# Modulation rows with moving weights, a first product in the setup stage, 64x64 blocks in the delta rule's inverse, and its dense tiles four units later

## The reference, cut to what matters

```
lower = where(strict, einsum('bhncd,bhnmd->bhncm', k_beta, k) * decay, 0.0)
a_mat = lower + eye(C)
sol = triangular_solve(a_mat, concat([v_beta, k_beta * exp(g)]), lower=True, unit_diagonal=True)
u, w = sol[..., :DV], sol[..., DV:]
...
step: v_new = u_i - w_i S;  o_i = q_dec_i S + qk_i v_new;  S = S * gl_i + k_dec_i^T v_new
```

## Time and profile before

| what | before |
|---|---|
| median of three runs | 3587.12 us |
| the profiled execution | 3585.75 us, its span 3583.9 us |
| TensorE (PE) matmuls busy | 3501.8 us, 98% |
| VectorE (DVE), ScalarE (ACT) busy | 1992.3 us (56%), 1233.8 us (34%) |
| mean granted TensorE clock | 0.991 of full speed |

### The profile page before, as it was taken

How to read it: one execution, slowest core, us unless ns; L and a number is a source line. 1 busy time by engine, 2 the same in 40 slices (tenths; PEclk the granted TensorE clock), 3 DMA queues, 4 the chain that set the end, 5 groups by cost and what they waited for, 6 DMA issues and landing times. The chain is left out here.

```text
span 3583.9 us, 43286 instructions
## 1 busy us (share of the span) xinstructions
PE 3501.8 (98%) x17750; PEld 2870.8 (80%) x17750; DVE 1992.3 (56%) x2959; ACT 1233.8 (34%) x1912; POOL 150.0 (4%) x212
## 2 busy tenths in 40 slices
PE   7999999999999999999999999999999999999999
PEld 6888877688888888877688887888888888888887
DVE  5665676775466755676763356665423376562233
ACT  3213334632233223344532234635322264442222
POOL 1110100001000100100000001000000000000000
PEclk8999999999999999999999999999999999999999
DMA  7663341245343653331343332211233222113322
GB/s 267 215 214 113 90 110 48 81 150 191 126 153 117 216 166 120 98 101 43 91 127 118 112 130 60 66 46 62 83 97 120 95 61 71 36 59 113 94 95 88
DMA packets 438042, 397.74 MB, mean 111 GB/s; under 512 B 53780, under 2 KB 390276, under 8 KB 437845
## 3 DMA queue, kind: packets, MB, share of 16 engines
q1 hardware_dynamic: 413028, 310.53, 28.5%
q0 software_dynamic: 24816, 84.45, 6.9%
HBM read 390.14 MB, written 4.78 MB: 110 GB/s over the span
## 5 line engine op out<-in xcount | busy, mean ns | idle before, releaser
L175 PE MATMUL m_ps<-m_h_high,ffn_w_high 128*128 128x512 f32 x2064 | 806.7, 391 | 2.9 <-DVE ffn_w_low L182 2.9
L177 PE MATMUL m_ps<-m_h_high,ffn_w_low 128*128 128x512 f32 x2064 | 803.5, 389 | 0.0
L176 PE MATMUL m_ps<-m_h_low,ffn_w_high 128*128 128x512 f32 x2064 | 803.2, 389 | 0.0
L1006 ACT ACTIVATE ffn_sil<-m_ps 128x512 f32<-128x512 f32 x132 | 79.1, 600 | 1095.1 <-PE m_ps L177 1095.1
L175 PEld LDWEIGHTS m_ps<-m_h_high,ffn_w_high 128*128 128x128 f32 x2064 | 387.5, 188 | 84.3 <-issue 4.3
L177 PEld LDWEIGHTS m_ps<-m_h_high,ffn_w_low 128*128 128x128 f32 x2064 | 387.4, 188 | 81.0
L176 PEld LDWEIGHTS m_ps<-m_h_low,ffn_w_high 128*128 128x128 f32 x2064 | 387.6, 188 | 79.1
L175 PE MATMUL m_ps<-ffn_w_high,ffn_hid_high 128*128 128x512 f32 x1056 | 411.6, 390 | 0.0
L177 PE MATMUL m_ps<-ffn_w_high,ffn_hid_low 128*128 128x512 f32 x1056 | 410.9, 389 | 0.0
L176 PE MATMUL m_ps<-ffn_w_low,ffn_hid_high 128*128 128x512 f32 x1056 | 410.9, 389 | 0.0
L182 DVE TENSOR_TENSOR ffn_w_low<-m_raw,ffn_w_high 128x2048 fp32r<-128x2048 f32 (+1 forms) x138 | 296.3, 2150 | 114.9 <-ACT ffn_w_high L1000 114.9
(11 more groups left out here) (498 smaller groups left out, 5497.6 us busy)
## 6 DMA issues: line engine op xcount, KB each, us to landing
m_raw<-in_ffn_w SPq DMA_DIRECT2D x176, 512.0 KB, 4.7
ffn_rows<-in_ada_w POOLq DMA_DIRECT2D x128, 512.0 KB, 5.1
ffn_rows<-in_ffn_w SPq DMA_DIRECT2D x88, 512.0 KB, 3.5
m_raw<-in_w_in SPq DMA_DIRECT2D x32, 1024.0 KB, 5.2
m_raw<-in_ffn_w_gate SPq DMA_DIRECT2D x44, 512.0 KB, 3.8
m_raw<-in_ffn_w_up SPq DMA_DIRECT2D x44, 512.0 KB, 4.9
ffn_rows<-in_ffn_w_down SPq DMA_DIRECT2D x44, 512.0 KB, 3.4
m_raw<-in_w_out SPq DMA_DIRECT2D x24, 512.0 KB, 4.6
```

The source lines that it names most:

```text
L175: pe.matmul(out, sh, mh, start=first, stop=False, skip_group_check=True)
L176: pe.matmul(out, sh, ml, start=False, stop=False, skip_group_check=True)
L177: return pe.matmul(out, sl, mh, start=False, stop=last, skip_group_check=True)
L1006: act.activation(sil[:, f % 2, :], M.ps[:, 2 * (f % 2), :], ACT.Silu).then_inc(S.silu_done, 1)
```

## The change: what it does

There are three edits in different stages, and one reordering.

1. **setup.** For chunks n = 2 and 3, VectorE sums only the first four slices (`on_dve(n)`). The other four are added by TensorE with the raw modulation weights as the moving operand and c broadcast as the stationary one, 128x512 each (`ada_products`); one more matmul with ones adds VectorE's part (`ada_rest`), ScalarE copies the one row (`copy_row`), and `ada_turn` turns it into columns. Seven tape heads instead of five stand ahead of the transposes. The gate weights of the first ffn tile are loaded after the first chunk's sum, and its first product (both halves, 48 matmuls of 256 columns) is done in setup, slice by slice as h comes; ffn begins with the up tile.
2. **scores** in mixer1_rest alternate between the two groups of rows.
3. **the inverse.** At levels 1 to 5 `first_product` and `updates` multiply only the two 64x64 blocks on the diagonal of each head (16 matmuls of 64x64 with 64 moving columns in place of 4 of 128x128 with 128), at level 6 one 64x64 block a head; copies and subtractions of level 6 are cut to that block, those of other levels stay whole.
4. **the tiles.** Tile n = 4 to 14 stands at unit 2(n - 4) + 5 instead of 2(n - 4) + 1, is evacuated in its own unit, ahead of that unit's `update`, and the last one (n = 15) stands behind the products u and w, its evacuation on ScalarE behind the last copy of w and on VectorE inside the recurrence.

```diff
+            def ada_products(n):
+                pe.wait_ge(ada_landed[2 * n + 1], 16)
+                for k in range(on_dve(n), DT):
+                    pe.matmul(row_bank(n), M.ccol[:, k:k + 1].to_broadcast([P, P]), ada[:, n, k, :], start=(k == on_dve(n)), stop=False)
+            def ada_rest(n):
+                pe.wait_ge(S.ada_partial, n + 1)
+                pe.matmul(row_bank(n), M.ones[:], part[:, n % 3, :], start=False, stop=True).then_inc(S.ada_rows, 1)
...
+            ada_products(2)
+            ada_rest(2)
+            ada_products(3)
             pe.wait_ge(S.mod_chain, 3)
-            ada_column(2)
-            ada_column(3)
+            ada_turn(2)
+            ada_rest(3)
+            keep_running(pe, M, 2, 2)
+            ada_turn(3)
+            pe.wait_ge(S.next_low, 1)
+            pe.wait_ge(S.h_ready, HALF)
+            first_product(range(HALF))
+            for k in range(HALF, DT):
+                if k > HALF:
+                    keep_running(pe, M, 2, 1)
+                pe.wait_ge(S.h_ready, k + 1)
+                first_product([k])
...
-                for h in range(HEADS):
-                    rows = slice(HD * (h // HPG), HD * (h // HPG + 1))
+                for a in range(HPG):
+                    for g in range(GROUPS):
+                        rows = slice(HD * g, HD * (g + 1))
...
+    final = len(sequence) - 1
+    last_unit = {n: 2 * (n - TT) + TT + 1 for n in range(TT, final)}
+    last_unit.update({n: -1 for n in range(TT - 1)})
+    ended = lambda u: [n for n in range(final) if last_unit.get(n) == u]
...
+        HALVES = [slice(0, P // 2), slice(P // 2, P)]
+        corner = lambda ap, h, half: head(ap[HALVES[half]], h)[:, HALVES[half]]
...
+                    elif n < LAST:
+                        for half in range(2):
+                            mm = pe.matmul(corner(out, h, half), corner(A.BT[:, i], h, half), corner(X[:, i], h, half), start=True, stop=True)
...
             for u in range(UNITS + 1):
                 if u < UNITS:
                     first_product(u)
-                if u % 2 and 4 + u // 2 < len(sequence) - 1:
-                    dense(4 + u // 2)
+                for n in ended(u):
+                    dense(n)
                 if u:
                     updates(u - 1)
                 if TT <= u - 2 < UNITS - TT:
                     turn_inverse(u - 2)
-            dense(len(sequence) - 1)
...
+            dense(final)
...
             for i in range(TT):
                 act.wait_ge(S.w_ready, i + 1)
                 act.copy(A.wT[:, i], M.ps[:, first_bank(UNITS + i) + 1]).then_inc(S.w_copied, 1)
...
-                high_gated(i)
+                if i < TT - 1:
+                    high_gated(i)
+            evacuate(final)
+            high_gated(TT - 1)
...
                 if i:
                     gate_output(i - 1)
                 else:
-                    low_gated(TT - 1)
+                    evacuate(final)
```

More of the change, by code:

```diff
@@ L232, in _ @@
             sp.dma_start(M.tri[:], const(nc, triangle(), "c_tri")).then_inc(S.tri_landed, 16)
-            sp.wait_ge(S.ada_partial, 2)
-            ahead.load(sp)
+            for s in range(2):
+                sp.wait_ge(S.ada_partial, s + 1)
+                ahead.load(sp, s)
             sp.wait_ge(S.ada_partial, 4)
@@ L281, in ada_column, with ada_turn, first_product @@
                 mm.then_inc(S.ada_column, 1)
+            def ada_products(n):
[5 more added lines that the diff above has]
+                pe.matmul(row_bank(n), M.ones[:], part[:, n % 3, :], start=False, stop=True).then_inc(S.ada_rows, 1)
+            def ada_turn(n):
+                c = order[n]
+                pe.wait_ge(S.row_copied, n - 1)
+                for q in range(T // P):
+                    mm = pe.matmul(M.ps[:, 7, 4 * c + q:4 * c + q + 1], part[0:1, row_slot(n), q * P:(q + 1) * P], M.ones[0:1, 0:1], start=True, stop=True)
+                mm.then_inc(S.ada_column, 1)
+            def first_product(ks):
+                for half in range(2):
+                    tokens = slice(2 * P * half, 2 * P * (half + 1))
+                    for k in ks:
+                        product(pe, M.ps[:, 0, tokens], (M.early[:, 0, k], M.early[:, 1, k]), (M.h_high[:, k, tokens], M.h_low[:, k, tokens]),
+                                k == 0 and half == 0, k == DT - 1)
             ada_column(0)
@@ L311, in _, with copy_row @@
             tape_copies(range(AT_ONCE, HEADS))
-            high_values(range(DT))
+            def copy_row(n):
+                act.wait_ge(S.ada_rows, n - 1)
+                act.copy(part[0:1, row_slot(n), :], row_bank(n)[0:1, :]).then_inc(S.row_copied, 1)
+            high_values(range(HALF))
+            copy_row(2)
+            ahead.first_high_act(act, M).then_inc(S.next_high, 1)
+            copy_row(3)
+            high_values(range(HALF, DT))
         @block.vector
@@ L2710, in first_product @@
                     pe.wait_ge(S.x_copied, u - 2 * TT + 1)
+                out = M.ps[:, first_bank(u)]
                 for h in range(DH):
-                    if n:
-                        mm = pe.matmul(head(M.ps[:, first_bank(u)], h), head(A.BT[:, i], h), head(X[:, i], h), start=True, stop=True)
-                    else:
-                        mm = pe.transpose(head(M.ps[:, first_bank(u)], h), head(A.BT[:, i], h), M.ident[:])
+                    if n == 0:
+                        mm = pe.transpose(head(out, h), head(A.BT[:, i], h), M.ident[:])
+                    elif n < LAST:
+                        for half in range(2):
+                            mm = pe.matmul(corner(out, h, half), corner(A.BT[:, i], h, half), corner(X[:, i], h, half), start=True, stop=True)
+                    else:
+                        mm = pe.matmul(head(out[HALVES[1]], h)[:, HALVES[0]], head(A.BT[HALVES[0], i], h)[:, HALVES[1]],
+                                       corner(X[:, i], h, 0), start=True, stop=True)
                 mm.then_inc(S.t1, 1)
@@ L2722, in updates @@
                 pe.wait_ge(S.t1_copied, u - TT + 1)
+                out = M.ps[:, first_bank(u)]
                 for h in range(DH):
-                    mm = pe.matmul(head(M.ps[:, first_bank(u)], h), head(T1[:, i], h), head(Y[:, i], h), start=True, stop=True)
+                    if n < LAST:
+                        for half in range(2):
+                            mm = pe.matmul(corner(out, h, half), corner(T1[:, i], h, half), corner(Y[:, i], h, half), start=True, stop=True)
+                    else:
+                        mm = pe.matmul(head(out[HALVES[0]], h)[:, HALVES[1]], head(T1[HALVES[1], i], h)[:, HALVES[0]],
+                                       corner(Y[:, i], h, 1), start=True, stop=True)
                 mm.then_inc(S.x_up, 1)
@@ L2868, in _ @@
                     copy_inverse(u - 2)
-                if u >= 3 and u % 2 and 4 + (u - 3) // 2 < len(sequence) - 1:
-                    evacuate(4 + (u - 3) // 2)
-                if u >= 5 and u % 2 and 2 + (u - 5) // 2 < len(sequence) - 1:
-                    square(2 + (u - 5) // 2)
-            evacuate(len(sequence) - 1)
+                for n in ended(u):
+                    evacuate(n)
+                for n in ended(u - 6):
+                    square(n)
             for i in range(TT):
@@ L2876, in _ @@
                 act.copy(A.wT[:, i], M.ps[:, first_bank(UNITS + i) + 1]).then_inc(S.w_copied, 1)
-                high_gated(i)
+                if i == 0:
+                    for u in range(UNITS - 6, UNITS):
+                        for n in ended(u):
+                            square(n)
+                if i < TT - 1:
+                    high_gated(i)
+            evacuate(final)
+            high_gated(TT - 1)
             act.wait_ge(ahead.landed[0], 16)
@@ L3006, in _ @@
                     mask(u + 2)
+                for n in ended(u):
+                    evacuate(n)
                 update(u)
-                n = 4 + (u - 3) // 2
-                if u >= 3 and u % 2 and n < len(sequence) - 1:
-                    evacuate(n)
-                if u >= 1 and u % 2 and 2 <= n - 1 < len(sequence) - 1:
-                    gated_convolution(n - 1, 0)
-                if u >= 2 and u % 2 == 0 and 2 <= n - 1 < len(sequence) - 1:
-                    gated_convolution(n - 1, 1)
-                if u >= 3 and u % 2 and 2 <= n - 2 < len(sequence) - 1:
-                    gated_convolution(n - 2, 2)
-            evacuate(len(sequence) - 1)
+                for n in ended(u):
+                    split_ahead(n)
+                for part in range(SCCONV):
+                    for n in ended(u - 2 - part):
+                        gated_convolution(n, part)
             def low_gated(c):
```

101 lines of the change are left out of this document (58 added, 43 removed).

## The result

The changed kernel takes 3594.77 us (median of 14 runs, 3588.35 to 3601.59) where the kernel before takes 3587.15 (14 runs, 3579.74 to 3591.49). The medians are 7.6 us apart. The ratio, which uses all runs, is 1.0027, with a 95% interval of 1.0019 to 1.0035: slower by 7 to 13 us. Forecast was 3588, range 3572 to 3622. The profiled execution of the changed kernel took 3588.35 us (span 3586.5), the least of its 14, so its stages are read one by one and not by their sum.

What follows compares the result with a forecast made beforehand. TensorE, busy 98% of the span, was taken as the bound. Per layer +3.6 us, two layers +7.2, opening -3.7, scores -2.5: +1.0 in all, giving 3588 us as the median; range 3572 to 3622.

Steps and rivals of the forecast that it cites:

- case "slower": Whole kernel slower than before, with about 7 us as the limit of telling a change; chance 0.43.
- first transposes to first product u: Delta stage, per layer: -19.7 blocks, +9.0 width changes, +10.0 idle first units, +2.5 clock, -1.5 waits, -1.1 last sum of squares.
- first product u to the stage's end: Delta stage's end: v_new 14.0 us behind first product u instead of 10.2, +3.8; with low_gated(3) together +4.4 us a layer.
- opening, whole kernel: Setup and first ffn tile: up tile starts at 54.7 instead of 58.43, -3.7 us; bounds -6 and +4.
- scores, whole kernel: Alternating row groups in mixer1_rest: sixteen records about 1.0 instead of 1.48 us, eight calls, -2.5 us; bounds 0 and -4.5.
- The blocks and the width: Inverse, per layer: 48 groups at 0.48 instead of 0.89 us, -19.7; 32 width changes at 0.28 us, +9.0.
- The rival that the pairs don't overlap: Inverse, levels 1 to 5: a group takes 0.96 instead of 0.48 us, 38 us more, 3626; chance 0.22.
- the rival of nearly free changes: Inverse: a pair of mode changes costs 0.08 instead of 0.28 us, 13 us less, 3575; chance 0.26.
- The first units: Delta stage's start: first dense tile waits for unit 5's mask, TensorE stands still 10.0 us of 12.1 a layer.
- the 2.5 us charged for the clock: Behind the first units' pauses, five us at half clock lose 2.5 us a layer; bounds 0 and 3.5.
- "-1.5, waits 4.0 against 5.5": Later units: the 1.34 us wait goes, TensorE waits 3.3 us for ScalarE at unit 25 plus 0.7 small; -1.5 a layer.
- The bound of 4 us more: Opening: if the clock stays down, ten matmuls take 17 us, up tile 4 us later, 3596; rival's chance 0.12.

Runs made afterwards that it cites:

- join_regroup: Changed kernel with the delta schedule of before, and in odd units the dense tile behind updates and transposes: 3559.50 us, ratio to before 0.9927.
- shift_only: Kernel before with only the later dense tiles, their evacuation in their own unit and the late last sum of squares, blocks whole: 3612.39 us, ratio 1.0066.
- after_again: The changed kernel run and profiled once more, nothing edited: 3596.28 us, ratio to before 1.0035.
- fillers: Changed kernel plus matmuls of 256 columns that nobody reads in three places where TensorE waits: 3590.54 us, ratio to before 1.0007.
- join_fill: Changed kernel with the delta schedule of before, plus 6 unread matmuls ahead of the 2.92 us wait for ScalarE's copy of unit 24: 3563.81 us, ratio 0.9944.

## Why the forecast came out as it did

The time, 3594.8, lies in the range, in the case "slower" and 7 us above the forecast. By its steps, in microseconds of a layer unless it says otherwise:

| term | forecast | measured |
|---|---|---|
| first transposes to first product u | -0.8 (the sum -19.7 + 9.0 + 10.0 + 2.5 - 1.5 - 1.1) | +0.1, -0.4 |
| first product u to the stage's end | +4.4 | +7.1, +7.2 |
| opening, whole kernel | -3.7 | -4.7 (interval -0.7 to -8.6) |
| scores, whole kernel | -2.5 | -1.8, not told from 0 |

**The blocks and the width.** Right in size: a unit was to take 0.44 + 2 x 0.48 + 0.28 = 1.68 us and takes 1.67. With 0.48 a group, 0.27 is left for the change of width in and out, and join_regroup, with 0.33 for a stretch fewer, bears that out. The rival that the pairs don't overlap is shown wrong, and the rival of nearly free changes too. The Trainium skill's page TensorEngine Tiling (Restrictions and Gotchas, Gotcha 1: PSUM Pressure) says that different row tiles can't access one PSUM bank at the same time; the two corners of a head lie in different rows and in different columns and write to one bank here, in different partitions, and pair by pair a group takes 0.5 us, where with the corners apart it takes 0.7 to 0.8, so the measurement decides against it for this case. The same page's drain at a change of mode (Tiling Modes, Key Properties) agrees, with 0.27 us.

**The first units.** Right: TensorE stands still or works at half clock there, 13.3 us where 12.9 was worked out, and the clock came back 2 us into the first dense tile. That tile took 6.7 us instead of 5.7. So the 2.5 us charged for the clock were too much: 0.4 and 1.0 were paid.

**Later units.** The step "-1.5, waits 4.0 against 5.5" failed. The wait of unit 25 was foreseen at 3.3 us and is 3.60, but with 0.68, 0.52 and twice 0.25 of others, for masks, it makes 5.30, more than the 3.88 of before (1.34, 1.97 and 0.57) and not less. Behind it the last two `updates` took 1.9 us at half clock instead of 1.0, which no term held. The sum of the stretch was nonetheless off by 0.9 and 0.4 us only, and that is luck: 1.1 us too much for the clock in the first units stood against 2.2 too little here.

**The stage's end** is the term that was mis-sized, +4.4 for +7.1. Its mechanism was right: `v_new` behind the roots. Where the clock stayed up, in the first layer of shift_only, both numbers came out, 14.0 us and +4.3. What was left out is the clock behind the wait of unit 25. The prediction charged lower clock to the first units alone; in the changed kernel the first three groups of products behind this wait took 4.8 us instead of 2.7. That is 14.0 + 2.1 = 16.1, the measured distance. From `v_new` to the end it is 1.3 us longer than before, 0.7 more than the 0.6 in the sum; a third stretch at half clock lies there, but no run separates it. The two layers make 5.5 us, and with the 0.9 and 0.4 above 6.8: the delta stage alone accounts for all that the forecast was short. Opening and scores together came near their sum of -6.2 (-6.5 by the ratios, with about 4 us of scatter each).

**The opening.** The bound of 4 us more did not come true in any profile; in the first profile the clock was up from 31 us on at the latest, so all ten matmuls ran at full speed, where about half of them had been charged at half; after_again shows the assumed case, with the up tile at 55.19, near the 54.7 of the prediction. So the term was too small in most executions: on average of the profiles the up tile starts 6.4 us earlier, not 3.7. A window that the prediction didn't read points to the reason: before, the clock was at 0.99 from 28 to 31 us, behind the transposes, and was at 0.50 from 31 us on, with the three tape heads and the pauses behind them. The changed kernel has one head there. That this is why the clock stays up in some executions and not in others isn't shown.

What stays open: the ratios of single parts carry about 4 us of scatter each, so whether opening and scores keep their full gain beside the other parts isn't shown. The delay's cost is split only by stretches of one trace (8.2 and 4.3 us), not by a run with the dense tiles delayed and the last sum of squares ahead of u and w, since that sum needs a convolution that ends later there.

## What to carry to other kernels

In this kernel independent dense tiles are the cover for a dependent chain: put them where the chain is slowest (here the masks of the first units), not where their own inputs are ready most comfortably; moving two tiles out of a place where VectorE was the bound, with the late last sum of squares, cost 13 us a layer, twice what the smaller blocks gave. Where a wait of 2 to 4 us opens on TensorE, count also the half clock that may come behind it, but only if TensorE is the bound in what follows. Put narrow groups next to each other, and an activation engine's table loads together, behind its last copy in a chain.

## What the runs showed of the hardware

- Two 64x64 matmuls in opposite corners of the array, with results in the two partition halves of one PSUM bank, overlap when issued one behind the other (16 records in about 0.5 us); with the corners in two series it is 0.7 to 0.8.
- The same pauses brought the clock down for longer in some executions than in others (0.97 against 0.92, 101.4 against 105.8 us, for the same stages of two executions of one program), so one profile of a kernel can lie 6 us under its median. It differs within one execution too: behind the same wait of unit 25, 2.41 us in both layers of shift_only, the clock stayed at 1.00 in the first and fell in the second.
- Filling the waits with matmuls held the clock at 1.00 in fillers and kept it at 0.86 instead of 0.50 in join_fill, and was worth 3.4 to 5.4 us a layer where TensorE's work followed and next to nothing (0.2 to 0.4) where VectorE and ScalarE set the pace.
